# Gate logits of a decoder trunk by split products with the gate's weights standing still

## The reference

```python
x = x + memory_cross_attention(h, m, w_xq, w_xk, w_xv, w_xo)
h = rmsnorm(x, norm_moe)
# the gate: 4 group logits and 32 expert logits for each token
g_logits = t @ w_group + b_group          # (2048, 4)
e_logits = t @ w_router + b_router        # (2048, 32)
# g_sel = argmax(g_logits); the top 2 experts in that group; gates from both
```

## Time and profile before

| what | value |
|---|---|
| median of 3 runs | 2660.02 us (2659.77 to 2660.62) |
| span of the profiled execution | 2659.8 us |
| mean granted clock of PE | 0.981 of full speed |
| stages | cross attention's steps from 1256 to 1696 us, routing to 1728 us, experts to about 2610 us |
| PE busy | 2536.7 us, 95% of the span |
| DVE busy | 1478.0 us, 56% |
| ACT busy | 1283.6 us, 48% |
| POOL busy | 602.4 us, 23% |

### The profile page before, as it was taken

How to read it: one execution, slowest core, us unless ns; L and a number is a source line. 1 busy time by engine, 2 the same in 40 slices (tenths; PEclk the granted TensorE clock), 3 DMA queues, 4 the chain that set the end, 5 groups by cost and what they waited for, 6 DMA issues and landing times. The chain is left out here.

```text
span 2659.8 us, 44805 instructions
## 1 busy us (share of the span) xinstructions
PE 2536.7 (95%) x14537; PEld 2053.6 (77%) x14539; DVE 1478.0 (56%) x1943; ACT 1283.6 (48%) x2286; POOL 602.4 (23%) x650
## 2 busy tenths in 40 slices
PE   9999999999999999989999999799999999999991
PEld 7888888676666678886888888688877888888881
DVE  5221344698888964444333332667888655565643
ACT  5221211698898931133222222346787645465543
POOL 0000011577777710000000000012222221121223
PEclk9999999999999999999999999799999999999996
DMA  7433240313201033243122121538999765576757
GB/s 267 167 119 127 75 166 25 100 45 144 65 18 45 2 127 111 99 152 112 62 82 85 73 87 48 200 130 326 386 379 367 267 220 200 191 279 205 253 161 271
DMA packets 141439, 414.83 MB, mean 156 GB/s; under 512 B 22016, under 2 KB 30720, under 8 KB 140288
## 3 DMA queue, kind: packets, MB, share of 16 engines
q1 hardware_dynamic: 125040, 371.15, 37.5%
q0 software_dynamic: 13968, 33.59, 5.3%
q10 hardware_dynamic: 2304, 8.39, 0.8%
HBM read 338.60 MB, written 91.75 MB: 162 GB/s over the span
## 5 line engine op out<-in xcount | busy, mean ns | idle before, releaser
L673 POOL TENSOR_TENSOR stick_weight<-stick_weight,stick_left 128x512 f32<-128x512 f32 (+3 forms) x320 | 327.8, 1038 | 126.9 <-DVE stick_left L805 122.4
L1820 DVE TENSOR_TENSOR moe_w_lo<-moe_w_lo_raw,moe_w_hi (+1 forms) x256 | 298.2, 1220 | 59.6 <-ACT moe_w_hi L1816 53.3
L1816 ACT CAST moe_w_hi<-moe_w_lo_raw (+1 forms) x256 | 255.7, 1052 | 48.2 <-DMA moe_w_lo_raw<-in_w 24.8
L805 DVE TENSOR_TENSOR_SCAN stick_left<-stick_z_ps,stick_left,stick_any_row 128x512 f32<-128x512 f32 x192 | 240.2, 1274 | 35.4 <-ACT stick_z_ps L768 35.1
L766 ACT ACTIVATE stick_weight<-stick_z_ps 128x512 f32<-128x512 f32 (+3 forms) x320 | 173.9, 543 | 32.8 <-PE stick_z_ps L715 21.1
L728 PE MATMUL stick_t_ps<-all_ident,stick_weight 128*128 128x128 f32 x1088 | 165.1, 281 | 19.0 <-ACT stick_weight_t L775 9.2
L768 ACT ACTIVATE stick_z_ps<-stick_z_ps 128x512 f32<-128x512 f32 (+3 forms) x320 | 165.7, 518 | 10.2
L728 PEld LDWEIGHTS stick_t_ps<-all_ident,stick_weight 128*128 128x128 f32 x1088 | 115.9, 141 | 70.0 <-issue 46.2
L64 PE MATMUL exp_g_ps<-moe_w_hi,exp_x_hi 128*128 x376 | 153.1, 407 | 7.1 <-DVE exp_x_lo L2224 7.1
L1831 POOL DMA_INDIRECT moe_xg<-hm_scratch,moe_now x50 | 62.4, 1247 | 412.6 <-PE exp_x_ps L2260 273.7
L64 PE MATMUL proj_z_ps<-proj_w_hi,proj_h_hi 128*128 128x512 f32 x384 | 151.9, 396 | 2.5 <-DVE proj_h_lo L392 2.5
(11 more groups left out here) (290 smaller groups left out, 5820.2 us busy)
## 6 DMA issues: line engine op xcount, KB each, us to landing
moe_w_lo_raw<-in_w SPq DMA_DIRECT2D x384, 512.0 KB, 13.0
proj_w_lo_raw<-in_w_in SPq DMA_DIRECT2D x40, 256.0 KB, 6.3
proj_xs<-in_x SPq DMA_DIRECT2D x16, 512.0 KB, 4.3
qt_scratch<-proj_qk_out SPq DMA_DIRECT2D x16, 512.0 KB, 2.8
kt_scratch<-proj_qk_out SPq DMA_DIRECT2D x16, 512.0 KB, 2.7
mix_q<-qt_scratch SPq DMA_DIRECT2D x16, 512.0 KB, 3.8
mix_out_xs<-in_x SPq DMA_DIRECT2D x16, 512.0 KB, 4.4
x_scratch<-mix_out_xs SPq DMA_DIRECT2D x16, 512.0 KB, 3.0
```

What stands on the lines that cost most here:

```text
L673: nc.gpsimd.tensor_tensor(taken, taken, after, ALU.mult).then_inc(weight_done, 1)
L805: nc.vector.tensor_tensor_scan(row[:, c * BANK:c * BANK + keys][:, ::-1], back, any_row[:, 0:keys], start, ALU.mult, ALU.bypass).then_inc( ...
L1816: nc.scalar.copy(self.w13_hi[:, self.w13_at(e, i)], self.w13_raw[:, self.w13_at(e, i)]).then_inc(self.w13_cut, 1)
L1820: ops.tensor_tensor(self.w13_lo[:, self.w13_at(e, i)], self.w13_raw[:, self.w13_at(e, i)], as_f32(self.w13_hi[:, self.w13_at(e, i)]), ALU. ...
```

## The change

The gate's weights are cut once into a high and a low part of type F32R and put side by side in `w_cut` (72 columns for each row of channels), ACT the high part and DVE the low one. Of each turned hm tile ACT writes the high part and DVE, in a new operation after it, the low part, into `hm_parts` (256 columns for each row: high, then low). PE runs one matmul for each of the 8 rows with `w_cut` standing and `hm_parts` moving; the result has 72 partitions and 256 columns. DVE copies it to `parts`, and PE runs two small fp32 matmuls with `parts` standing and `both_parts` (two stacked identities of 36) moving, which add the four sums and turn them back to tokens on partitions. DVE then adds the bias as before. `hm_parts` lies where the keys were, `w_cut` and `parts` where the turned hm was.

```diff
+        hm_parts = s.over("hm_parts", [P, rows, 2, P], F32R, key_at)
+        w_cut = s.over("w_cut", [P, rows, 2 * n_logit], F32R, ahead.work_at + 4 * 3 * width)
+        parts = s.over("parts", [2 * n_logit, 2, P], F32, ahead.work_at + 4 * (3 * width + 2 * rows * n_logit))
+        both_parts = s.sbuf("both_parts", [2 * n_logit, n_logit])
...
@@ gpsimd, before root(0)
+                nc.gpsimd.memset(both_parts[:], 0.0).then_inc(both_set, 1)
+                for part in range(2):
+                    pool.wait_ge(both_set, part + 1)
+                    nc.gpsimd.affine_select(out=both_parts[:], in_=both_parts[:], compare_op=ALU.not_equal, fill=1.0, base=-part * n_logit,
+                                            pattern=[[-1, n_logit]], channel_multiplier=1).then_inc(both_set, 1)
@@ scalar, after the first part's last turn
+                act.wait_ge(consts_loaded, 80)
+                act.wait_ge(vo_done, rows)
+                nc.scalar.copy(w_cut[:, :, 0:n_logit], w_logit[:]).then_inc(w_hi_cut, 1)
@@ scalar, step
-                            last = nc.scalar.copy(hm_t[:, cut], s_ps[:, cut])
+                            last = nc.scalar.copy(hm_parts[:, cut, 0], s_ps[:, cut])
@@ vector, after the first part's last turn
                 dve.wait_ge(consts_loaded, 80)
+                dve.wait_ge(w_hi_cut, 1)
+                nc.vector.tensor_tensor(w_cut[:, :, n_logit:], w_logit[:], as_f32(w_cut[:, :, 0:n_logit]), ALU.subtract).then_inc(w_cut_done, 1)
@@ vector, step
                     if there(b, 2) and not is_first(b):
                         low_x(b + 2)
+                    if there(b, -1):
+                        dve.wait_ge(mt_out, b)
+                        wait_past(dve, logit_done, b - 1)
+                        for cut in halves:
+                            last = nc.vector.tensor_tensor(hm_parts[:, cut, 1], s_ps[:, cut], as_f32(hm_parts[:, cut, 0]), ALU.subtract)
+                        last.then_inc(ml_out, 1)
                     if there(b, 1):
                         dve.wait_ge(exped, b + 2)
...
                     if there(b, -1):
                         dve.wait_ge(logit_done, b)
+                        wait_past(dve, parts_added, b - 1)
+                        nc.vector.tensor_copy(parts[:], h_ps[0:2 * n_logit, 1:3]).then_inc(parts_out, 1)
+                        dve.wait_ge(parts_added, b)
                         nc.vector.tensor_tensor(logits[:, bass.ds(b - 1, 1), :], h_ps[:, 0:1, 0:n_logit],
@@ tensor, before the steps
-                pe.wait_ge(consts_loaded, 80)
+                pe.wait_ge(w_cut_done, 1)
+                pe.wait_ge(both_set, 3)
@@ tensor, step
                     if there(b, -1):
-                        pe.wait_ge(mt_out, b)
+                        pe.wait_ge(ml_out, b)
...
-                            last = nc.tensor.matmul(h_ps[:, 0, 0:n_logit], hm_t[:, r], w_logit[:, r], start=r == 0, stop=r == rows - 1)
+                            last = nc.tensor.matmul(h_ps[0:2 * n_logit, 1:3], w_cut[:, r], hm_parts[:, r], start=r == 0, stop=r == rows - 1)
                         last.then_inc(logit_done, 1)
                     if there(b, 1):
...
-                        wait_past(pe, mt_out, b)
+                        wait_past(pe, ml_out, b)
                         transposes(s_ps, p_sb, tp_done)
+                    if there(b, -1):
+                        pe.wait_ge(parts_out, b)
+                        for part in range(2):
+                            last = nc.tensor.matmul(h_ps[:, 0, 0:n_logit], parts[:, part], both_parts[:], start=part == 0, stop=part == 1)
+                        last.then_inc(parts_added, 1)
```

More of the change, by code:

```diff
@@ L1254, in __init__ @@
         self.xs = s.sbuf("cross_xs", [P, 2, w_q.shape[1]])
+        self.work_at = s.next_at()
         self.work = s.sbuf("cross_work", [P, 4, w_q.shape[1]])
@@ L1270, in load_first, with attend_memory @@
             self.load_wo(sp, n)
-def attend_memory(nc, x1, gain_q, ahead, key_t, value_t, gain_moe, w_group, w_router, b_group, b_router,
+def attend_memory(nc, x1, gain_q, ahead, key_t, value_t, key_at, gain_moe, w_group, w_router, b_group, b_router,
                   ident, half, x2, hm, logits, consts):
@@ L1303, in attend_memory @@
         p_sb, x2_sb, hm_sb = work[:, 0], work[:, 1], work[:, 2]
-        hm_t = work[:, 3].rearrange("p (r t) -> p r t", t=P)
+        hm_parts = s.over("hm_parts", [P, rows, 2, P], F32R, key_at)
+        w_cut = s.over("w_cut", [P, rows, 2 * n_logit], F32R, ahead.work_at + 4 * 3 * width)
+        parts = s.over("parts", [2 * n_logit, 2, P], F32, ahead.work_at + 4 * (3 * width + 2 * rows * n_logit))
+        both_parts = s.sbuf("both_parts", [2 * n_logit, n_logit])
         p_hi, p_lo = p_parts[:, 0], p_parts[:, 1]
@@ L1318, in attend_memory @@
                  "res_loaded x2_stored hm_stored squared meaned rooted h_done ht_done hh_done hl_done scored maxed negated exped "
-                 "inverted p_done tp_done ph_done pl_done xo_done added m_squared m_meaned m_rooted hm_done tm_done mt_out "
-                 "logit_done logit_out picked")
+                 "inverted p_done tp_done ph_done pl_done xo_done added m_squared m_meaned m_rooted hm_done tm_done mt_out ml_out "
+                 "logit_done logit_out picked both_set w_hi_cut w_cut_done parts_out parts_added")
         (consts_loaded, gains_loaded, wt_done, wt_act, wt_dve, sk_done, sk_cut, sk_ready, vo_done, vo_cut, vo_ready,
          res_loaded, x2_stored, hm_stored, squared, meaned, rooted, h_done, ht_done, hh_done, hl_done, scored, maxed, negated, exped,
-         inverted, p_done, tp_done, ph_done, pl_done, xo_done, added, m_squared, m_meaned, m_rooted, hm_done, tm_done, mt_out,
-         logit_done, logit_out, picked) = (s.sem(n) for n in names.split())
+         inverted, p_done, tp_done, ph_done, pl_done, xo_done, added, m_squared, m_meaned, m_rooted, hm_done, tm_done, mt_out, ml_out,
+         logit_done, logit_out, picked, both_set, w_hi_cut, w_cut_done, parts_out, parts_added) = (s.sem(n) for n in names.split())
         halves = [slice(0, rows // 2), slice(rows // 2, rows)]
@@ L2420, in build_trunk @@
                 c = Scope(nc, crossing, "kv")
+                key_at = c.next_at()
                 key_t, value_t = c.sbuf("key_t", [P, rows, slots]), c.sbuf("value_t", [P, rows, slots])
@@ L2423, in build_trunk @@
                 project_memory(nc, memory, w_xk[0], w_xv[0], ident[:], consts, key_t, value_t, ahead, tiles)
-                picks = attend_memory(nc, x1, norm_cross[0], ahead, key_t, value_t, norm_moe[0], w_group[0], w_router[0],
+                picks = attend_memory(nc, x1, norm_cross[0], ahead, key_t, value_t, key_at, norm_moe[0], w_group[0], w_router[0],
                               b_group[0], b_router[0], ident[:], half, x2, hm, logits, consts)
```

## The result

The changed kernel takes 2675.94 us (median of 5 runs, 2673.81 to 2677.25) beside 2660.62 us for the kernel before: a ratio of 1.0053, with a 95% interval of 1.0042 to 1.0064. The two medians are 15.3 us apart; the ratio makes it 14.1. The forecast was 2675.4 us. The profiled execution is the shortest of the five, 2673.81 us with a span of 2672.1, so its differences from the trace of before (span 2659.8) add up to 12.3 us, not to 15.

What follows compares the result with a forecast made beforehand. PE, always busy at full clock, was taken to bound the cross-attention steps, with engines working one after the other at both stage ends. Terms -5.2 + 0 + 3.5 + 2.1 + 11.4 + 3.6 = +15.4 on 2660.02 gave 2675.4 us, range 2668 to 2683.

Steps and rivals of the forecast that it cites:

- PE's work in a step: Gate logits in 13 middle steps: 1.82 us removed, 0.96 and 0.46 added, 0.40 gained a step, 5.2 in all.
- Not late by DVE: Middle steps: DVE's copy of the sums ends at 0.9 us, PE's transposes at about 1.0, so small matmuls do not wait.
- The rival in which PE gains nothing: Middle steps: small matmuls wait 0.3 us for DVE's copy, product a little slower than 0.120; 2680.6 us, 14 in 100.
- Step 14: First of the last steps: earlier product, but bias add waits for the small matmuls and the low part runs as now; 0 us.
- The start: Scores of tile 0: PE waits for DVE's cut of the gate weights; 3.5 us lost, bounds 2.9 and 4.
- The clock: After PE's new idle time at tile 0's scores the granted clock falls; 2.1 us lost, bounds 0 and 3.4.
- the second of the two cases: Clock estimate at the start: 0.52 mean clock over 1665 to 1672, PE losing half of 5.75 busy us, 2.8.
- Steps 15 and 16: End of the stage: DVE's new wait stands ahead of the choice of experts; 11.4 us and 3.6 us lost.
- The rival on the other side, that the choices stay hidden: Steps 15 and 16: DVE's choice of 14 tiles still ends near 1678.8; 8 in 100 no difference, 2 faster.
- a sign with some 14 us: Step 15: DVE would stand idle some 14 us ahead of the new subtraction if the forecast is right.
- that rival's world: Choices hidden in steps 15 and 16, only the chain longer: 2663.3 us, or 2657.7 if the weights' cut is hidden too.
- The sum: Whole kernel: -5.2 + 0 + 3.5 + 2.1 + 11.4 + 3.6 = +15.4 us on the median, 2675.4 us, slower by 0.6%.

Runs made afterwards that it cites:

- experiment 8: Changed kernel with choices ahead of the subtraction in steps 15 and 16 and PE's wait moved to the first logits, the eight product matmuls run twice: 2676.35 us.
- experiment 7: Changed kernel with choices ahead of the subtraction in steps 15 and 16 and PE's wait moved to the first logits, the two small matmuls run twice: 2667.1 us.
- experiment 2: Changed kernel with PE's wait for the cut gate weights and both_parts moved from tile 0's scores to the first logits in step 1: 2670.23 us, ratio 1.0027.
- experiment 6: Changed kernel with 14 identity matmuls on PE while it waits for the gate weights' cut ahead of tile 0's scores: 2673.48 us, ratio 1.0041.
- experiment 1: Changed kernel with DVE's wait for ACT's copy and the subtraction moved behind the choice of experts in steps 15 and 16: 2665.32 us, ratio 1.0014.
- experiment 4: Kernel before plus one DVE wait for ACT's copy of turned hm ahead of the choice of experts in steps 15 and 16: 2672.64 us, ratio 1.004.
- experiment 3: Changed kernel with both edits: choices ahead of the subtraction in steps 15 and 16, PE's wait moved to the first logits: 2659.36 us, ratio 0.999.

## Why the prediction was right

**PE's work in a step: right in kind, 0.02 us off.** 0.38 us gained for 0.40. The product shows 1.05 us instead of 0.96, since I took eight spacings and no border, though the 1.82 us that I took off had theirs in it (the sixteen loads last 1.98 us there and 1.86 at 1682.18, where no long matmul stands ahead of them); experiment 8 gives the spacing as 0.1175, near the 0.120 of the earlier trace rows. Other parts of a step came out shorter than I had them: the small matmuls take 0.44 us (experiment 7) for 0.46, the scores 10.79 instead of 10.82 from first load to next load, and the turning of the softmax weights 0.88 instead of 0.91. So part of the closeness is errors that cancel.

As for the rule of the Trainium skill, "TensorE: Matmul & The Clock Gate", section "Back-to-back issue gap": it gives an isolated matmul of 256 columns 262 cycles at 2.4 GHz, an estimated 0.109 us. The runs do not agree; they show 0.1175. The section "LDWEIGHTS (loading the stationary operand)" has a load's time go with the columns: a single load's duration is 141 ns for 72 columns here (median of 128) and 192 for the 128 columns of the old logits, in that direction, but the spacing hardly gains by it, 0.1175 us with 72 columns and 0.120 with 128.

**Not late by DVE: right.** The copy takes 0.42 us (0.4 taken) and ends 0.15 us ahead of the small matmuls. The rival in which PE gains nothing needed this margin to be used up, and in none of the 13 steps does the trace show PE idle there.

**Step 14: no gain by the chain, as said,** and DVE's cut of the softmax weights starts 3.92 us behind the first load of the logits (1661.61 to 1665.53), where it was 4.14. That is 0.2 us of the -1.3 of the account. The other 1.1 are the clock's: in the output product of tile 15 it was low for some 5.7 us before (the earlier trace rows has 0.52 over 1665 to 1672) and for some 3.4 us after (0.76 over the same window). It varies between executions and nothing ties it to the change: the product starts behind 2.68 us of idle time both in the changed kernel and in experiment 2, and the latter has full clock there.

**The start: 3.4 us for 3.5.** DVE's cut of 288 columns took 0.45 us as estimated. **The clock: 1.3 for 2.1,** the term that was most mis-sized: the fall came in the scores of tile 0 and lasted less there than in the second of the two cases in the earlier trace rows. Experiments 2 and 6 show that in this place it hangs on the idle time.

**Steps 15 and 16: 11.4 for 11.4 and 3.5 for 3.6.** The rival on the other side, that the choices stay hidden, had its point in the time at which DVE's choice of 14 tiles ends. It ends at 1693.55 where it had to end near 1678.8. DVE's idle time ahead of the subtraction, named as a sign with some 14 us, is 12.77. Experiments 1 and 4 show it from both sides: take the wait from ahead of the choice and 10.6 us come back; put only the wait there and 11.1 are lost. The price I set on that rival's world, 2663.3 with PE's wait left at the start and 2657.7 without, turned out as 2665.3 and 2659.4, about two microseconds dearer; by the marks 1.2 of them are step 16, where that price took the choice to be hidden and experiment 3 shows it in the way of the subtraction.

**The sum.** 15.4 us forecast; 15.3 between the medians, 14.1 by the ratio (2660.62 times 0.0053), 12.3 between the two traces. The forecast's own terms come to 13.3 in the traces, 1.3 less for step 14 and 0.8 less for the clock than it had; -2.1 us behind the steps and +1.1 ahead of them are none of its terms. So the mechanism and the large terms are confirmed, but that the median lies within 0.6 us of the forecast is luck: the changed kernel's own runs spread over 3.4 us. What shortens the stretch behind the steps stays open.

## What to carry to other kernels

When a new wait goes into an engine's program, read what stands behind it in the prologue and the last rounds and not in the steady ones only: here 13 steps hid it for nothing and gained 5 us, and one round without the covering work paid 11. Put a wait right ahead of what needs it: moving two waits, with no work removed, turned a loss of 14 to 15 us into a gain of 2. Then look at each round again, since the order that is right for one may cost another: the choice ahead of the subtraction gave back 9.3 us in step 15 and held the chain up by 1.3 in step 16. A later bias add together with a hand-over by halves, where the engines form a chain, gave 3 to 4 more.

## What the hardware showed beside it

The timed runs of one kernel spread over 3 to 5 us (2660.12 to 2664.05 in 23 runs of the kernel before). The traces of before and after differ by 1.1 us at DVE's last cut of `vo`, with 1.7 of it in a stretch of low granted clock that one execution has and the other has not; experiment 1's trace, with the same operations there, has full clock (1.00 from 1193.5 to 1200), yet stands 1.6 us later than the trace of before at the same cut, by differences further ahead. A claim about 1 us needs the marks of a trace, not the medians.

The same idle time of PE does not always bring the low clock. Ahead of the output product of tile 15 it is 2.68 us in the changed kernel and in experiment 2; behind it the granted clock is 0.50 from 1668 to 1671 in the one and 1.00 from 1664.9 to 1671 in the other. Ahead of the experts PE is idle for 3.40 us before and 3.41 after, with 1.00 behind it in the one trace (1728 to 1731) and 0.70 in the other (1741.7 to 1744.7). So a forecast of a clock term needs a range and not a value.
